# Two transformer blocks in one kernel: the shared expert's gate and up products are put behind single slots of the second expert group

## What is computed

```
t = h.reshape(-1, d)                                  # 256 + 16 tokens; the kernel does the 256
g_idx  : best of 4 groups per token
e_idx  : best 2 of the 8 experts of that group, with weights
a, b   = t @ w_gate[e], t @ w_up[e]                   # 32 experts, 1024 -> 256
routed = sum over e of (silu(a) * b * combine[e]) @ w_down[e]      # 256 -> 1024
shared = (silu(t @ w_sh_gate) * (t @ w_sh_up)) @ w_sh_down         # every token
out    = routed + shared
```

## Time and profile before

| | |
|---|---|
| runs | 738.94 us median of 3 (738.7 to 742.1) |
| profiled execution | 737.79 us, its span 736.0 us |
| PE | busy 667.2 us, 91% of the span |
| DVE, ACT, POOL | 331.8, 280.9, 46.9 us |
| chain that ended last | PE 66%, DMA 19%, DVE 7%, ACT 4% |
| HBM | 180.48 MB read, 247 GB/s over the span |
| mean granted clock of TensorE | 0.960 |

### The profile page before, as it was taken

How to read it: one execution, slowest core, us unless ns; L and a number is a source line. 1 busy time by engine, 2 the same in 40 slices (tenths; PEclk the granted TensorE clock), 3 DMA queues, 4 the chain that set the end, 5 groups by cost and what they waited for, 6 DMA issues and landing times.

```text
span 736.0 us, 10953 instructions
## 1 busy us (share of the span) xinstructions
PE 667.2 (91%) x4473; PEld 517.5 (70%) x4473; DVE 331.8 (45%) x607; ACT 280.9 (38%) x529; POOL 46.9 (6%) x68
## 2 busy tenths in 40 slices
PE   8999899898677895778889999999989999999996
PEld 5979787734212741133359999989789999999994
DVE  8676555631101011011056566647755544445554
ACT  7655563312001010011055666573555433344432
POOL 1000102000001000000037200000000000000000
PEclk9999999999777999688999999999999999999998
DMA  9926309599999959999995444335525455455201
GB/s 355 419 92 228 115 8 420 231 364 415 423 420 421 403 217 422 423 420 420 423 420 205 172 145 143 115 123 197 196 104 183 172 183 211 179 174 192 93 1 58
DMA packets 26145, 182.23 MB, mean 248 GB/s; under 512 B 3040, under 2 KB 3168, under 8 KB 4464
## 3 DMA queue, kind: packets, MB, share of 16 engines
q1 hardware_dynamic: 25344, 178.81, 62.1%
q10 hardware_dynamic: 752, 2.73, 0.9%
HBM read 180.48 MB, written 1.05 MB: 247 GB/s over the span
## 4 chain that ended last, share of the span: by engine, by line
PE 66%; DMA 19%; DVE 7%; ACT 4%; issue 2%; POOL 1%; SPq 0%; DVEq 0%; POOLq 0%; ACTq 0%
PE ps L1377 64%; DMA ring<-stream_dram 18%; PE ps L1380 2%; DVE ring_r L362 2%; ACT single L355 1%; DMA vec<-small_dram 1%; DVE work L1331 1%; ACT work L768 1%; DVE work L1334 0%; DVE turned L1290 0%; POOL stat L810 0%; DVE turned L1350 0%; POOL stat L872 0%; ACT work L696 0%; ACT turned L773 0%
## 5 line engine op out<-in xcount | busy, mean ns | idle before, releaser
L1377 PE MATMUL ps<-turned,single 128*128 128x256 f32 (+1 forms) x1312 | 240.1, 285 | 2.9 <-DVE turned L1350 1.2
L1377 PEld LDWEIGHTS ps<-turned,single 128*128 128x128 f32 x1312 | 203.0, 189 | 6.0 <-issue 2.9
L1377 PE MATMUL ps<-turned,ring_r 128*128 128x256 f32 (+1 forms) x656 | 185.5, 283 | 0.0
L362 DVE TENSOR_TENSOR ring_r<-ring,single 128x1024 fp32r<-128x1024 f32 x134 | 160.8, 1243 | 49.4 <-ACT single L355 49.4
L1377 PE MATMUL ps<-ring,work 128*32 128x512 f32 (+2 forms) x814 | 134.1, 666 | 32.9 <-DMA ring<-stream_dram 28.5
L355 ACT ACTIVATE single<-ring 128x1024 fp32r<-128x1024 f32 x134 | 133.8, 1049 | 2.2 <-DMA ring<-stream_dram 1.7
L1377 PEld LDWEIGHTS ps<-turned,ring_r 128*128 128x128 f32 x656 | 124.0, 189 | 0.0
L1377 PEld LDWEIGHTS ps<-ring,work 128*32 128x32 f32 (+1 forms) x814 | 38.1, 127 | 107.9 <-DMA ring<-stream_dram 62.5
L1377 PE MATMUL ps<-single 128*128 128x512 f32 (+1 forms) x299 | 64.6, 363 | 3.6 <-DVE single L1244 2.0
L1377 PEld LDWEIGHTS ps<-single 128*128 128x128 f32 x299 | 47.0, 197 | 28.8 <-issue 15.6
L1377 PE MATMUL ps<-single,turned 128*128 128x512 f32 (+3 forms) x208 | 59.8, 365 | 3.1 <-DVE turned L1054 1.8
(11 more groups left out here) (227 smaller groups left out, 576.3 us busy)
## 6 DMA issues: line engine op xcount, KB each, us to landing
ring<-stream_dram SPq DMA_DIRECT2D x161, 1024.0 KB, 11.8
work<-stream_dram SPq DMA_DIRECT2D x5, 1024.0 KB, 13.0
turned_w<-stream_dram SPq DMA_DIRECT2D x2, 1024.0 KB, 13.6
gain<-gains_dram ACTq DMA_DIRECT2D x3, 512.0 KB, 8.2
cst<-consts_dram ACTq DMA_DIRECT2D x1, 1066.0 KB, 9.0
h<-x_dram SPq DMA_DIRECT2D x2, 512.0 KB, 4.1
out_dram<-work SPq DMA_DIRECT2D x4, 256.0 KB, 2.0
vec<-small_dram SPq DMA_DIRECT2D x1, 451.5 KB, 5.8
```

Of the source, the lines that this page charges most:

```text
L362: dve.tensor_tensor(ring_r[:, place, a], ring[:, place, a], w_hi[k % HIGHS][:, a].bitcast(F32), ALU.subtract).then_inc(s["wlo_done"], 1)
L1377: return pe.matmul(o, lhsT, rhs, start=start, stop=stop, **kw)
```

## The change

The shared expert's gate slot goes behind slot t=2 of the second pair of group 1 (position 53) and its up slot behind t=5 (position 57). The down slot comes behind the group (position 64), with the turning before it. The order of the stream follows. Gate and up are added up in banks 6 and 7, not 4 and 5, and the turning uses bank 4. ScalarE's and VectorE's work on them stands ahead of their work on the second pair. TensorE's wait for `hs_done` moves ahead of the pair's down products. GpSimd's memsets wait for `used` = `ASIDE_END` = 29, not 62.

```
+SHARED_GROUP = 1
+SHARED_BEHIND = {2: 0, 5: 1}
+SH_GATE_AT = MOE_AT + SHARED_GROUP * MOE_GROUP + Q_SLOTS + 3
+SH_UP_AT = SH_GATE_AT + 4
+SH_DOWN_AT = MOE_AT + (SHARED_GROUP + 1) * MOE_GROUP + 2
...
+            shared = {SH_GATE_AT: SH_GATE, SH_UP_AT: SH_UP, SH_DOWN_AT: SH_DOWN}
+            return shared[n] if n in shared else n + 3 - sum(at < n for at in shared)
...
-                    act.activation(sg_s[:, i, :], ps[:, 4 + i, 0:FF], ACT.Silu, scale=rsb[:, i:i + 1]
+                    act.activation(sg_s[:, i, :], ps[:, 6 + i, 0:FF], ACT.Silu, scale=rsb[:, i:i + 1]
...
                 for p in range(PAIRS):
+                    if shared and p == PAIRS - 1:
+                        shared_silu()
                     act.wait_ge(s["gu_ps"], it * PAIRS + (p + 1))
...
-            pool.wait_ge(used, SHARED_AT)
+            pool.wait_ge(used, ASIDE_END)
...
                 for p in range(PAIRS):
+                    if shared and p == PAIRS - 1:
+                        shared_hidden()
                     dve.wait_ge(s["sg_done"], it * PAIRS + (p + 1))
...
-                dve.tensor_copy(hs, halves(ps[:, 6, :], TOK)).then_inc(s["hst_sb"], 1)
+                dve.tensor_copy(hs, halves(ps[:, 4, :], TOK)).then_inc(s["hst_sb"], 1)
...
+            def shared_gate_up(b):
+
+                n = (SH_GATE_AT, SH_UP_AT)[b]
+                slot_ready(pe, n)
+                for i in range(NT):
+                    for t in range(DT):
+                        last = mm(ps[:, 6 + i, b * FF:(b + 1) * FF], tT[:, t, i * P:(i + 1) * P],
+                                  home(n)[:, t * FF:(t + 1) * FF], t == 0, t == DT - 1)
+                        if i == t == 0:
+                            last.then_inc(used, 1)
+                    if b:
+                        last.then_inc(s["sgu_ps"], 1)
...
                         if t == 1 and p:
                             scatter(p - 1, 1)
+                        if shared and p and t in SHARED_BEHIND:
+                            shared_gate_up(SHARED_BEHIND[t])
...
+                    if shared and p:
+                        pe.wait_ge(s["hs_done"], NT)
                     down(p)
...
-                moe_group(g, g, early_slot(g) if g < SHARED_GROUP else moe_slot(g), used, g == 0)
-                if g == SHARED_GROUP - 1:
-                    shared_gate_up()
+                moe_group(g, g, early_slot(g), used, g == 0, g == SHARED_GROUP)
+                if g == SHARED_GROUP:
                     shared_turned()
                     shared_down()
```

More of the change, by code:

```diff
@@ L69 @@
 MOE_AT = B1 - 3
-SHARED_GROUP = 2
-SHARED_AT = MOE_AT + SHARED_GROUP * MOE_GROUP
+SHARED_GROUP = 1
[3 more added lines that the diff above has]
+SH_DOWN_AT = MOE_AT + (SHARED_GROUP + 1) * MOE_GROUP + 2
 ASIDE, ASIDE_WORK = 7, 5
@@ L373, in entry_at @@
         def entry_at(n):
-            if n < MOE_AT or n >= SHARED_AT + 3:
+            if n < MOE_AT or n > SH_DOWN_AT:
                 return n
-            return n + 3 if n < SHARED_AT else SH_GATE + n - SHARED_AT
+            shared = {SH_GATE_AT: SH_GATE, SH_UP_AT: SH_UP, SH_DOWN_AT: SH_DOWN}
+            return shared[n] if n in shared else n + 3 - sum(at < n for at in shared)
         def place2(n):
@@ L658, in shared_silu, with moe_group @@
                     act.wait_ge(s["sgu_ps"], i + 1)
-                    act.activation(sg_s[:, i, :], ps[:, 4 + i, 0:FF], ACT.Silu, scale=rsb[:, i:i + 1]
+                    act.activation(sg_s[:, i, :], ps[:, 6 + i, 0:FF], ACT.Silu, scale=rsb[:, i:i + 1]
                                    ).then_inc(s["ssg_done"], 1)
-            def moe_group(it):
+            def moe_group(it, shared=False):
                 for t in (0, 1, 4, 5):
@@ L678, in _ @@
             for g in range(LOOPED):
-                moe_group(g)
-                if g == SHARED_GROUP - 1:
-                    shared_silu()
+                moe_group(g, g == SHARED_GROUP)
             act.wait_ge(s["rounds_done"], 1)
@@ L1213, in shared_hidden, with shared_rows, moe_group @@
                     dve.wait_ge(s["ssg_done"], i + 1)
-                    dve.scalar_tensor_tensor(hs_tok[:, i, :], ps[:, 4 + i, FF:2 * FF], rsb[:, i:i + 1], sg_s[:, i, :],
+                    dve.scalar_tensor_tensor(hs_tok[:, i, :], ps[:, 6 + i, FF:2 * FF], rsb[:, i:i + 1], sg_s[:, i, :],
                                              ALU.mult, ALU.mult).then_inc(s["hs_done"], 1)
+            def shared_rows():
                 dve.wait_ge(s["hst_ps"], 1)
-                dve.tensor_copy(hs, halves(ps[:, 6, :], TOK)).then_inc(s["hst_sb"], 1)
-            def moe_group(it, ranks=None, ahead=None, first=False):
+                dve.tensor_copy(hs, halves(ps[:, 4, :], TOK)).then_inc(s["hst_sb"], 1)
+            def moe_group(it, ranks=None, ahead=None, first=False, shared=False):
                 for t in (2, 6):
@@ L1249, in _ @@
                 moe_group(g, rankp[:, :, g * PER_GROUP:(g + 1) * PER_GROUP],
-                          rankp[:, :, (g + 1) * PER_GROUP:(g + 2) * PER_GROUP], g == 0)
-                if g == SHARED_GROUP - 1:
-                    shared_hidden()
+                          rankp[:, :, (g + 1) * PER_GROUP:(g + 2) * PER_GROUP], g == 0, g == SHARED_GROUP)
+                if g == SHARED_GROUP:
+                    shared_rows()
             dve.wait_ge(s["rounds_done"], 1)
@@ L1643, in _ @@
             mm(ps[:, 2, 2 * E:3 * E], ones, chosen[:, 1, :], False, True).then_inc(s["rank_ps"], 1)
[L1645 to L1657, removed]
+            def shared_gate_up(b):
[9 more added lines that the diff above has]
+                        last.then_inc(s["sgu_ps"], 1)
             def shared_turned():
-                pe.wait_ge(s["hs_done"], NT)
                 for f in range(FF // P):
                     for i in range(NT):
-                        last = turn(ps[:, 6, f * TOK + i * P:f * TOK + (i + 1) * P], hs_tok[:, i, f * P:(f + 1) * P])
-                        if f == i == 0:
-                            last.then_inc(used, 1)
+                        last = turn(ps[:, 4, f * TOK + i * P:f * TOK + (i + 1) * P], hs_tok[:, i, f * P:(f + 1) * P])
                 last.then_inc(s["hst_ps"], 1)
             def shared_down():
-                slot_ready(pe, SHARED_AT + 2)
+                slot_ready(pe, SH_DOWN_AT)
                 pe.wait_ge(s["hst_sb"], 1)
@@ L1674, in shared_down, with moe_group @@
                             last = mm(ps[:, 2 * i + n, :], hs[:, f, i * P:(i + 1) * P],
-                                      home(SHARED_AT + 2)[:, f * D + n * 512:f * D + (n + 1) * 512], False, False,
+                                      home(SH_DOWN_AT)[:, f * D + n * 512:f * D + (n + 1) * 512], False, False,
                                       skip_group_check=True)
                 last.then_inc(used, 1)
-            def moe_group(it, g, moe_slot, freed, first=False, ending=False):
+            def moe_group(it, g, moe_slot, freed, first=False, shared=False, ending=False):
                 def keep_warm(p):
@@ L1789, in ready @@
                     n = MOE_AT + g * MOE_GROUP + k
+                    if g == SHARED_GROUP:
+                        n += sum(k >= Q_SLOTS + t + 1 for t in SHARED_BEHIND)
                     slot_ready(pe, n)
```

## The result

The changed kernel took 730.23 us (median of 4 runs, 728.3 to 731.2) beside 739.33 for the kernel before (738.7 to 742.1): a ratio of 0.986, 95% interval 0.983 to 0.989. Measured again on another occasion it took 729.81 (729.28 to 730.17) beside 739.93, ratio 0.986 (0.983 to 0.988). The prediction was 730.0.

What follows compares the result with a forecast made beforehand. The weight stream bounds the MoE stage, with a ring stall at the shared expert; -9.7 + 0.4 + 0.4 = -8.9 us gives 728.9 for the profiled execution and 730.0 for the median, range 728.4 to 733.9.

Steps and rivals of the forecast that it cites:

- The stall as the whole of the gain: MoE stage, ring dip between 250 and 270 us: the whole 9.7 us lost there comes back.
- what the last group gains, the end gains: Behind position 108 nothing waits for the stream, so time gained by the last group is gained at the end.
- The schedule: TensorE's work laid out anew in groups 1 and 2: gate begins at 214.7, position 65 is passed at 256.6.
- The number: Whole kernel: 728.9 us for the profiled execution, 730.0 for the median of the runs.
- The margin: Refill of position 65, a slot free at 256.6, must be issued by 259.7: 3.1 us to spare.
- The catching up by position 63: Group 1's last down slot lands at 239.5, the three ahead are done by 238.1: TensorE has caught up there.
- The lost rate: Transfer of position 73, issued with about 4.7 us of transfers ahead: 0.4 us taken, between nothing and 1.0.
- The clock: TensorE's clock may drop during gate, leaving 2.4 us of delay and some 1 us lost; 0.4 taken on average.
- The cover of silu and product, and the memsets: Shared silu and product run under slots t=6 and t=7: 0; GpSimd's memsets move into group 0: 0.
- B: Stall returns in part at the head of group 2, TensorE 3 to 7 us late: 733.9 us, chance 0.15.
- C: Clock stays at 1.2 GHz through both products and what follows: 763 us, chance 0.03.
- D: Stall goes but the end does not move, as something else ends the MoE stage late: 738 us, chance 0.07.

Runs made afterwards that it cites:

- The first experiment: Changed kernel with only two of the eight steps of the shared gate and up products multiplied: 729.79 us, ratio 0.987.
- The idle products: Changed kernel with 11, 22 or 43 idle products ahead of the turning of the shared hidden rows: 732.47, 734.94 and 740.49 us.
- both late: Changed kernel with gate behind slot t=5 and up behind t=6 of the pair: 735.0 us, ratio 0.992.
- Two edits that each looked 1.0 to 1.5 us faster: Changed kernel with memsets back at group 1's end (728.33 us), or three idle products for four in group 3's last pair (728.76); both together 728.92.

## Why the prediction was right

- **The stall as the whole of the gain.** Counted as 9.7 us in the windows and 9.9 in the slots. Between positions 53 and 108 the changed kernel took 9.3 and 7.9 us less in its two profiles; the sum had -8.9. Right, to 1 us, and so is "what the last group gains, the end gains": 374.9 us behind position 108 before, 374.8 and 374.7 after. The first experiment excludes that 10 us of TensorE's work ahead of position 63 are worth more than the 2 to 3 us by which runs differ.
- **The schedule.** Laid out: position 65 passed at 256.6 when gate begins at 214.7. In the second profile of the changed kernel gate begins at 214.68 and the first slot of group 2 at 255.88, against the "near 256" of the prediction. Gate, three slots, up and two slots take 18.98 us in the first profile; 18.7 was laid out. Position 108 was missed: "near 351.5" was said, 353.23 came in the second profile, with gate at the forecast 214.7. The sum had no term for TensorE falling behind the stream in group 3's last pair, where the idle products leave it 2.12 us a slot; that was 1.6 us in this execution and 0.5 in the first.
- **The number.** The profiled execution was to take 728.9; the two profiled took 731.2 and 729.7. The medians came to 730.2 and 729.8 for 730.0. Single executions of the changed kernel lie between 728.3 and 731.2, so agreement to 0.2 us is in part luck; what the traces support is 8 to 9 us of gain.
- **The margin.** 3.1 us laid out, some 2 found. The prediction let the refill be issued as soon as the slot is passed; by the changed kernel's own trace position 65 is passed with the begin of the second slot, near 259.4, and the issue stands at 260.56, about 1 us later. For the down slot (252.0) it had counted that delay, for position 65 it had not. The idle products show still less: 0.3 to 1.0 us of their delay is swallowed in the stage, nothing of it in the medians. The change stands nearer to the edge than the prediction said.
- **The catching up by position 63.** In the first profile TensorE waits 1.14 us for it at 242.42. (The prediction's own times leave 239.5 - 238.1 = 1.4 there, of which its term for the clock used 1.0.) In the second, where gate took longer, the four down slots run without a wait from 237.15, and the first slot of group 2 comes 41.2 us after position 53 for 40.9. So TensorE has caught up or nearly. That this, and not the distance between the products, is what the place has to give, up next to gate (no difference) and both late (5.0 us slower) show.
- **The lost rate.** 0.4 us taken, 398 GB/s in one window is 0.5.
- **The clock.** 0.4 us taken. In the first profile the drop came before gate (0.57 from 212 to 216), and gate ran at 1.00; in the second it fell into gate: 0.63 from 214 to 218, and the run of 104 records took 20.53 us for 18.98, 1.55 us more, of which the wait for position 63 took most; 0.3 us reached the first slot of group 2 and 0.3 us position 76. So the size was right there. Seven further profiles have gate at this place and up behind it: in one the run took 20.53 us, in six 18.84 to 18.98, and in one of the six, up stood next to gate. In the late version the same kind of drop cost 3.6 us of TensorE's time and found no wait to hide in.
- **The cover of silu and product, and the memsets.** Both at 0. The first: VectorE's second half ended at 235.25 + 0.49 = 235.7, under the slots that ran to 236.6; right. The memsets: not shown to be anything else, and not settled below 1.5 us. The late begin of the first profile is not theirs: they start at 168.12, behind the run of six slots at 166.15 that was late already.
- **The rivals.** B, a stall that returns at the head of group 2, did not come here, but it is what every slower variant shows, at the place and of the kind described. C (1.2 GHz throughout) and D (the end does not move) did not come.

## What to carry to other kernels

In this kernel's stage, whose weights stream through a ring, a long product costs nothing as long as the engine has caught up with the stream before the next stretch without slots to pass; beyond that each further microsecond cost 0.8 to 1.0 us in the stage. So look for the window in which the transfers dip, count the bytes that it lacks, and spread the work so that each piece is followed by enough slots to catch up; as long as that holds, it matters little between which slots it stands (behind t=3 or behind t=5 made no difference). Leave slack for the clock: in a stretch where the engine mostly waited it fell just ahead of such a product or within it in three profiles, and cost 1.6, 1.6 and 3.6 us of TensorE's time. And when you delay an engine on purpose, read the length of the delay from the trace before you reckon with it.

## What the runs showed that was not expected

- In the first profile the stream held 2.484 us a slot over 23 slots, with two 7 us products between them. A transfer issued with some 2 us to spare over the 4.7 of an empty queue still landed in time.
- The same kernel's gate product met the clock's drop in one profile (20.53 us for 104 records; 0.63 from 214 to 218 us) and missed it in another (18.98; 0.57 from 212 to 216 us, ahead of gate): the drop comes at another point of the program from one execution to the next.
- Two edits that each looked 1.0 to 1.5 us faster in medians of 4 and 6 runs gave nothing together. Differences of 0.2% are below what such runs tell, even where, as here, the ranges of two single measurements do not overlap (728.10 to 728.78 against 729.28 to 730.17).
